# Feed-forward layers: one load of 512 moving columns for the high and low activations, in place of two of 256

## What is computed

```python
def _ffn(h, p):                                                # first stack
    return (jax.nn.silu(h @ p['w_ff_gate']) * (h @ p['w_ff_up'])) @ p['w_ff_down']

gate, up = jnp.split(h2 @ w_gate_up[l], 2, axis=-1)            # second stack
x = x + (jax.nn.silu(gate) * up) @ w_down[l]
```

## Time and profile before

| what | value |
|---|---|
| median of 3 runs | 2888.91 us (2883.22 to 2889.05) |
| the profiled execution's own time | 2887.15 us |
| its span, first to last instruction | 2885.4 us |
| TensorE matmul / weight load, busy share | 93% / 89% |
| VectorE / ScalarE, busy share | 71% / 53% |
| mean granted TensorE clock | 0.962 of full |

### The profile page before, as it was taken

The page is one execution under the profiler, slowest core; times in us unless marked ns, Lnnn a source line. Parts: engine busy times, 40 slices in busy tenths (PEclk is TensorE's granted clock), DMA queues, the critical chain, the costliest instruction groups (busy, mean ns, idle before and its releaser), DMA issues.

```text
span 2885.4 us, 66260 instructions
## 1 busy us (share of the span) xinstructions
PE 2691.2 (93%) x27300; PEld 2555.8 (89%) x27300; DVE 2037.8 (71%) x3675; ACT 1518.7 (53%) x3207; POOL 0.2 (0%) x4
## 2 busy tenths in 40 slices
PE   7989899999989899899989898999999899998998
PEld 5988889999988779799989887798998689996998
DVE  4987878688778887666658788877665665565655
ACT  4555355655655346454565453465445555455554
POOL 0000000000000000000000000000000000000000
PEclk9999999999999999999999899999999999999999
DMA  8453445455554334355434433344554145541554
GB/s 297 151 190 131 140 151 183 144 177 185 165 178 146 132 125 161 119 190 185 151 97 161 147 113 114 104 151 174 183 186 136 63 133 178 187 160 38 165 184 157
DMA packets 120500, 442.32 MB, mean 153 GB/s; under 512 B 13296, under 2 KB 15472, under 8 KB 118816
## 3 DMA queue, kind: packets, MB, share of 16 engines
q1 hardware_dynamic: 108416, 392.86, 40.7%
q10 hardware_dynamic: 11808, 45.42, 4.6%
HBM read 437.18 MB, written 1.05 MB: 152 GB/s over the span
## 4 chain that ended last, share of the span: by engine, by line
PE 67%; DVE 20%; ACT 6%; DMA 3%; issue 2%; SPq 0%; ACTq 0%; DVEq 0%
PE lin L462 17%; PE lin L463 17%; PE lin L464 17%; DVE arena L1869 5%; DVE w_lo L1709 5%; DMA w_raw<-in_stream 2%; ACT w_hi L1109 2%; PE lin L475 1%; PE lin L478 1%; PE lin L479 1%; DMA a_raw<-in_ada 1%; PE aux L580 1%; PE aux L663 1%; PE lin L513 1%; PE aux L642 1%
## 5 line engine op out<-in xcount | busy, mean ns | idle before, releaser
L1709 DVE TENSOR_TENSOR w_lo<-w_raw,w_hi 128x1024 fp32r<-128x1024 f32 x722 | 876.3, 1221 | 332.3 <-ACT w_hi L1109 326.7
L462 PE MATMUL lin<-h_hi,w_hi 128*128 128x256 f32 x3456 | 1001.3, 290 | 5.3 <-DVE h_lo L1805 2.9
L463 PE MATMUL lin<-h_lo,w_hi 128*128 128x256 f32 x3456 | 988.6, 286 | 0.0
L464 PE MATMUL lin<-h_hi,w_lo 128*128 128x256 f32 x3456 | 988.0, 286 | 0.0
L1109 ACT ACTIVATE w_hi<-w_raw 128x512 fp32r<-128x512 f32 x1446 | 828.8, 623 | 261.1 <-DMA w_raw<-in_stream 164.5
L462 PEld LDWEIGHTS lin<-h_hi,w_hi 128*128 128x128 f32 x3456 | 673.7, 195 | 15.8 <-issue 5.3
L463 PEld LDWEIGHTS lin<-h_lo,w_hi 128*128 128x128 f32 x3456 | 673.6, 195 | 0.2
L464 PEld LDWEIGHTS lin<-h_hi,w_lo 128*128 128x128 f32 x3456 | 672.9, 195 | 0.0
L462 PE MATMUL lin<-s_hi,w_hi 128*128 128x256 f32 x1520 | 441.0, 290 | 11.1 <-DVE s_lo L1805 4.5
L464 PE MATMUL lin<-s_hi,w_lo 128*128 128x256 f32 x1520 | 432.6, 285 | 0.5 <-issue 0.5
L463 PE MATMUL lin<-s_lo,w_hi 128*128 128x256 f32 x1520 | 433.1, 285 | 0.0
(11 more groups left out here) (279 smaller groups left out, 3495.5 us busy)
## 6 DMA issues: line engine op xcount, KB each, us to landing
w_raw<-in_stream SPq DMA_DIRECT2D x723, 512.0 KB, 3.6
a_raw<-in_ada ACTq DMA_DIRECT2D x80, 512.0 KB, 3.6
arena<-in_first SPq DMA_DIRECT2D x6, 1024.0 KB, 14.0
X<-in_tokens SPq DMA_DIRECT2D x2, 1024.0 KB, 13.5
s_f<-in_first SPq DMA_DIRECT2D x2, 1024.0 KB, 18.3
arena<-in_const ACTq DMA_DIRECT2D x1, 1856.0 KB, 10.2
arena<-in_small ACTq DMA_DIRECT2D x1, 1536.0 KB, 13.3
out<-arena SPq DMA_DIRECT2D x1, 1024.0 KB, 3.9
```

The lines of the kernel that those rows point to most:

```text
L462: used(pe.matmul(o, whi, hi[:, k, :], start=k == 0, stop=False), first)
L463: pe.matmul(o, whi, lo[:, k, :], start=False, stop=False)
L464: mm = pe.matmul(o, wlo, hi[:, k, :], start=False, stop=k == kcs - 1)
L1709: dve.tensor_tensor(w_lo[:, m % SLOTS, :], w_raw[:, m % RAW, :], w_hi[:, m % SLOTS, :].bitcast(F32), ALU.subtract).then_inc(sems["lo_ready ...
```

## The change

In four of the five feed-forward parts (passes two and four and both layers of the second stack) high and low activations lie in one tensor (`h_both`, `s_both`), and for each weight tile TensorE makes two matmuls: the high weights by both parts at once (512 columns, a whole bank), and the low weights by the high part (256 columns, into the bank's first half). What was one sum in a bank is now two halves, MAIN and CROSS, that have to be added. For a pair of chunks ScalarE copies both CROSS halves (512 elements), VectorE adds both MAIN halves to them and frees the two banks, and only then ScalarE applies SiLU, in place in SBUF. VectorE splits the product of a pair one pair later. For a down chunk VectorE does one more operation (CROSS out by ScalarE, MAIN added by VectorE, then the residual). The first pass keeps three products. Pairs need an even bank, so in pass four two dummy matmuls that keep the clock are now a chunk of the ring (`keep_clock_in_ring`), and ScalarE's `post` waits for it before its first operation. In every feed-forward part the running sum is now made in the second half alone.

```diff
...
+            def two_halves(o, both, k, last):
+
+                whi, wlo, first = weight()
+                mm = pe.matmul(o.rearrange("p (a t) -> p a t", a=2), whi, both[:, :, k, :], start=k == 0, stop=False)
+                return mm, first, pe.matmul(o[:, MAIN], wlo, both[:, 0, k, :], start=False, stop=last)
+
+            def dense_halves(both, ready=None, kcs=KC):
+
+                o = bank()
+                for k in range(kcs):
+                    if ready:
+                        pe.wait_ge(sems[ready[0]], ready[1] + k + 1)
+                    mm, first, end = two_halves(o, both, k, k == kcs - 1)
+                    used(mm, first)
+                done(end)
...
-            def post(l, x, b, squared=False):
-
-                warm()
+            def post(l, x, b, squared=False, ring=False):
+
+                if ring:
+
+                    arrived(0)
+                    moved(act.activation(small[:, 1, 14:15], c1("alpha")[:, 1:2], ACT.Sqrt))
+                else:
+                    warm()
...
+            def feed_forward_halves(gate, squared=None):
+                for i in range(2):
...
+                    for c in range(HALF):
+                        cross = arrived_pair()
+                        if c >= 2:
+
+                            act.wait_ge(sems["s_ready"], s0 + c - 1)
+                        act.activation(two_bufs[:, :, c % 2, :], cross, ACT.Copy).then_inc(sems["cross_moved"], 1)
+
+                        act.wait_ge(sems["lin_evac"], n.at("lin_evac"))
+                        act.activation(gate_buf[:, c % 2, :], gate_buf[:, c % 2, :], ACT.Silu).then_inc(sems["pair_silu"], 1)
+                        split_to(at.tile // TILES + SLOTS)
...
+            def residual_halves(x, alpha, gate, means, early):
+
+                for c in range(KC):
+                    lows_for(1)
+                    o, buf = at.next_bank(), gate_buf[:, c % 2, :]
+                    dve.wait_ge(sems["cross_moved"], at.up("cross_moved"))
+                    if gate is None:
+                        ins = dve.tensor_tensor(buf, o[:, MAIN], buf, ALU.add)
+                    else:
+                        ins = dve.scalar_tensor_tensor(buf, o[:, MAIN], gate(c), buf, ALU.mult, ALU.add)
+                    ins.then_inc(sems["lin_evac"], 1)
+                    dve.wait_ge(sems["lin_evac"], at.up("lin_evac"))
+                    dve.scalar_tensor_tensor(x[:, c, :], x[:, c, :], alpha, buf, ALU.mult, ALU.add).then_inc(sems["r_ready"], 1)
...
+            def feed_forward_halves(x, gate):
...
+                    for c in range(HALF):
+                        lows_for(2)
+                        main, pair, y = at.next_pair(MAIN), two_bufs[:, :, c % 2, :], y_buf[:, c % 2, :]
+                        dve.wait_ge(sems["cross_moved"], at.up("cross_moved"))
+                        dve.tensor_tensor(pair, main, pair, ALU.add).then_inc(sems["lin_evac"], 2)
+                        dve.wait_ge(sems["lin_evac"], at.up("lin_evac", 2))
+                        if c:
+                            split_product(c - 1)
+                        dve.wait_ge(sems["pair_silu"], at.up("pair_silu"))
+                        step(dve.tensor_tensor(y, gate_buf[:, c % 2, :], y, ALU.mult))
+                    split_product(HALF - 1)
...
```

More of the change, by code:

```diff
@@ L339, in v2, with bank_pair @@
             return vec2[:, at:at + 1]
-        lin = [ctx.enter_context(nc.psum_tensor(f"lin{i}", [P, 512], F32)) for i in range(4)]
+        lin_banks = ctx.enter_context(nc.psum_tensor("lin", [P, 4, 512], F32))
+        lin = [lin_banks[:, i, :] for i in range(4)]
+        def bank_pair(b, cols):
+            assert b % 2 == 0
+            return lin_banks[:, b:b + 2, cols]
+        MAIN, CROSS = slice(0, S), slice(S, 2 * S)
         aux = [ctx.enter_context(nc.psum_tensor(f"aux{i}", [P, 512], F32)) for i in range(4)]
@@ L465, in dense, with dense_halves_together @@
                 done(mm)
+            def two_halves(o, both, k, last):
[10 more added lines that the diff above has]
+                done(end)
+            def dense_halves_together(chunks, ready):
+                banks, start = [bank() for _ in range(chunks)], at.tile
+                for k in range(KC):
+                    pe.wait_ge(sems[ready[0]], ready[1] + k + 1)
+                    for c, o in enumerate(banks):
+                        at.tile = start + c * KC + k
+                        mm, first, end = two_halves(o, h_both, k, k == KC - 1)
+                        used(mm, first if c == 0 else k == KC - 1)
+                        if k == KC - 1:
+                            done(end)
             def dense_together(chunks, ready):
@@ L606, in keep_clock, with keep_clock_in_ring @@
                     pe.matmul(aux[3][:, 0:S], c1("mean1024"), const1[:, 0:S], start=True, stop=True)
+            def keep_clock_in_ring(k):
+                o = bank()
+                for _ in range(k):
+                    mm = pe.matmul(o[:, 0:S], c1("mean1024"), const1[:, 0:S], start=True, stop=True)
+                done(mm)
             def head_columns(name, heads, chunks):
@@ L693, in feed_forward @@
                     for c in range(KC):
-                        dense(s_hi, s_lo, ("s_ready", s0) if c == 0 else None, kcs=HALF)
+                        ready = ("s_ready", s0) if c == 0 else None
+                        if halves:
+                            dense_halves(s_both, ready, kcs=HALF)
+                        else:
+                            dense(s_hi, s_lo, ready, kcs=HALF)
                     n.up("r_ready", KC)
-                    n.up("sum_ready")
+                n.up("sum_ready")
             def gates(l):
@@ L962, in _ @@
                     else:
-                        keep_clock(2)
+                        if turn == 3:
+                            keep_clock_in_ring(2)
+                        else:
+                            keep_clock(2)
                         variance_columns(M)
@@ L976, in _ @@
                     n.up("h_ready", KC)
-                    feed_forward()
+                    feed_forward(turn > 0)
                     if turn == 3:
@@ L1117, in arrived, with arrived_pair @@
                 at.tile_done = at.tile
+                if at.freed_elsewhere:
+                    act.wait_ge(sems["lin_evac"], n.at("lin_evac"))
+                    at.freed_elsewhere = False
                 n.up("lin_evac")
                 return at.next_bank()
+            def arrived_pair():
+                for _ in range(2):
+                    at.tile += KC
+                    split_to((at.tile - 1) // TILES + SLOTS)
+                    act.wait_ge(sems["lin_done"], at.up("lin_done"))
+                    at.tile_done = at.tile
+                n.up("lin_evac", 2)
+                return at.next_pair(CROSS)
             def moved(ins):
@@ L1834, in residual @@
                         early(c)
+            def residual_halves(x, alpha, gate, means, early):
+                for c in range(KC):
+                    lows_for(1)
[3 more added lines that the diff above has]
+                        ins = dve.tensor_tensor(buf, o[:, MAIN], buf, ALU.add)
+                    else:
+                        ins = dve.scalar_tensor_tensor(buf, o[:, MAIN], gate(c), buf, ALU.mult, ALU.add)
+                    ins.then_inc(sems["lin_evac"], 1)
+                    dve.wait_ge(sems["lin_evac"], at.up("lin_evac"))
+                    dve.scalar_tensor_tensor(x[:, c, :], x[:, c, :], alpha, buf, ALU.mult, ALU.add).then_inc(sems["r_ready"], 1)
+                    n.up("r_ready")
+                    if means and c >= 1:
+                        dve.wait_ge(sems["r_ready"], at.now("r_ready"))
+                        ins = dve.tensor_tensor(std[:, 1, :], std[:, 1, :] if c > 1 else x[:, 0, :], x[:, c, :], ALU.add)
+                        if c < KC - 1:
+                            step(ins)
+                        else:
+                            ins.then_inc(sems["sum_ready"], 1)
+                            n.up("sum_ready")
+                    early(c)
@@ new lines, in feed_forward_halves, with split_product @@
+            def feed_forward_halves(x, gate):
+                scaled = gate is not None
+                def split_product(c):
+                    both_parts(s_hi[:, c, :], s_lo[:, c, :], y_buf[:, c % 2, :], "s_ready")
+                dve.wait_ge(sems["lin_evac"], n.at("lin_evac"))
+                at.bank = n.at("lin_evac") % 4
+                for i in range(2):
+                    for c in range(HALF):
[9 more added lines that the diff above has]
+                    split_product(HALF - 1)
+                    dve.wait_ge(sems["r_ready"], at.now("r_ready"))
+                    residual_halves(x, ALPHA if scaled and i == 0 else 1.0, gate, scaled and i == 1, lambda c: None)
+                dve.wait_ge(sems["r_ready"], at.now("r_ready"))
@@ L1849, in feed_forward @@
                     dve.wait_ge(sems["r_ready"], at.now("r_ready"))
```

(2 more changed lines are left out.)

60 lines of the change are left out of this document (45 added, 15 removed).

## The result

The changed kernel takes 2868.41 us in the median of 4 runs (2863.09 to 2870.81), beside 2888.98 (2883.22 to 2890.86) for the kernel before on the same chip: a ratio of 0.9934, with a 95% interval of 0.9919 to 0.9948. That is 20.6 us less. The forecast was 2849, 40 us less: the sign was right and the size twice too large. 2868 is what the first rival gave. The profiled execution took 2863.09 us, with a span of 2861.3.

The account below looks back on a forecast made before the run. TensorE's matmul distances were taken to bound the kernel. -47.1 + 3.8 + 2.0 + 1.2 = -40.1 us from the profiled 2887.15 gave 2847.0; with the median 1.8 above that execution, 2849 us, range 2824 to 2872.

Parts of the forecast that it names:

- the first rival: Feed-forward tiles: each weight load adds its own 13.3 ns, wide matmul 0.227 us; 21.1 us less, 2868; chance 0.20.
- What bounds the kernel: Four feed-forward parts: TensorE is busy for all of 190 us at full clock; nobody else sets the pace.
- Two matmuls for three: Feed-forward tiles: wide 0.217, narrow 0.120, so 0.337 instead of 0.360 us; 2048 tiles, 47.1 us less.
- the four rows it stood on: Trace evidence on matmul distances: half clock, full clock at 0.120 us, 48 weight columns, and plain float32 dummies.
- From gate and up to down: First down chunk: TensorE waits at the eleventh tile for VectorE, 0.48 us eight times; 3.8 us more.
- Leaving a part: Last down chunk: one more VectorE operation before the residual, 0.51 us four times; 2.0 us more at most.
- Pass four's norm: Pass four: ScalarE's table load waits for the dummies, now a chunk of the ring; 1.2 us more.
- Costs beside TensorE and the handover: Chunk pairs: VectorE 4.27, ScalarE 3.55, loop 5.0 us fit within 5.39; rival of a longer loop: 2921, chance 0.10.
- The sum: Whole kernel: -47.1 + 3.8 + 2.0 + 1.2 = -40.1 us.

Follow-up runs that it names:

- three loads again: The changed kernel with the wide matmul cut back into two of 256 columns, three loads a tile, all else kept: 2888.10 us, ratio 0.9999 to the kernel before.
- TensorE alone: Runs without the reference's computation, in blocks of 64 matmuls of one kind at full clock: fp32r distances 0.1199, 0.1733 and 0.2267 us for 256, 384 and 512 columns.

## Why the prediction was wrong, by its own steps

**What bounds the kernel** was right: TensorE's distances, and nothing else. The saved matmul with its load moved the parts; everything else of the change together moved nothing that shows (three loads again: 0.9999).

**Two matmuls for three: the term that failed.** It took 0.217 for the wide matmul and 2048 x 0.023 = 47.1 us. Measured are 0.233 and 0.117, a saving of 13.3 or 6.7 ns a tile by its pace: 758 x 0.0133 + 1285 x 0.0067 = 18.7 us. The step that failed is the sentence that a load "fits nearly free into 213 ns, and does not quite fit into 107". TensorE alone shows the same 13.3 ns with 256, 384 and 512 columns, so nothing of it is hidden by a longer stream, and in the kernel the wide one stands at 0.230 to 0.241. Three of the four rows it stood on were of another kind. The dummies in plain float32 have another type, whose surplus is 2.7 ns. The half clock has no surplus for either form, as the first tiles of the last part show now, where the granted clock is 0.50:

```profile
2662.25 0.63 PE L487 MATMUL lin<-h_both,w_hi 128*128 128x512 f32 x1
2662.67 0.41 PE L488 MATMUL lin<-h_both,w_lo 128*128 128x256 f32 x1
2662.89 0.47 PE L487 MATMUL lin<-h_both,w_hi 128*128 128x512 f32 x1
```

Wide 0.42, narrow 0.22, together 768 columns at 1.2 GHz: at half clock the change gains nothing. And the 48 weight columns tell nothing of 128, since the surplus does not go with the columns loaded. The row that did count, 0.120 at full clock with the right type and load, gave the first rival: 13.3 ns for each load, 2868. Its mean is close; its constancy is not, since a tile of wide and narrow has two paces. That its 2868 was met so closely is in part luck: it had 27.3 us saved in the tiles and 6.2 given back, where 18.7 and 1.7 were measured.

**From gate and up to down: oversized.** Forecast 0.48 us eight times, 3.8. The chain, second stack, VectorE, ScalarE and TensorE:

```profile
2394.88 0.40 PE L487 MATMUL lin<-s_both,w_hi 128*128 128x512 f32 x1
...
2395.08 0.60 ACT L1320 ACTIVATE two_bufs<-lin 128x512 f32<-128x512 f32 x1 [1.68 <-PE lin L488]
2395.78 0.69 DVE L1990 TENSOR_TENSOR two_bufs<-lin,two_bufs 128x512 f32<-128x512 f32 x1 [1.00 <-ACT two_bufs L1320]
...
2397.17 0.42 DVE L1995 TENSOR_TENSOR two_bufs<-two_bufs 128x256 f32<-128x256 f32 x1
2397.62 0.29 DVE L1921 CAST s_both<-two_bufs 128x256 fp32r<-128x256 f32 x1
2397.95 0.42 DVE L1922 TENSOR_TENSOR s_both<-two_bufs,s_both 128x256 fp32r<-128x256 f32 x1
...
2398.43 0.50 PE L487 MATMUL lin<-s_both,w_hi 128*128 128x512 f32 x1
2398.77 0.28 PE L488 MATMUL lin<-s_both,w_lo 128*128 128x256 f32 x1
```

The last part is ready at 2398.37, 3.49 after the first down tile's start; the forecast had 3.59. But the eleventh tile comes later than forecast, at 10 x 0.353 = 3.53, and TensorE, which has just worked, starts 0.06 behind VectorE and not 0.26. Its next start is 0.34 later instead of 0.23. The eleventh tile's distance from the tenth and the twelfth's from it are together 0.12 to 0.19 us longer than two at 0.353; over all eight stalls that is 1.2 us.

**Leaving a part: 2.0 forecast at most, 0.5 measured.** It shows in pass four alone, where the mean's first matmul starts 2176.52 - 2174.56 = 1.96 us after ScalarE takes out the last chunk, beside 1.45 before. In the second stack ScalarE's squares wait behind a weight split in either kernel; in pass two the next low part is waited for either way (3.08 and 3.10 us from last start to next).

```profile
2174.56 0.47 ACT L1331 ACTIVATE two_bufs<-lin,mod 128x256 f32<-128x256 f32 x1 [1.38 <-PE lin L488]
...
2175.07 0.48 DVE L1962 SCALAR_TENSOR_TENSOR two_bufs<-lin,mod,two_bufs 128x256 f32<-128x256 f32 x1
2175.59 0.42 DVE L1965 SCALAR_TENSOR_TENSOR X<-X,two_bufs 128x256 f32<-128x256 f32 x1
...
2176.52 0.70 PE L737 MATMUL aux<-std,const 128*128 128x256 f32 x2 [2.00 <-DVE std L1969]
```

**Pass four's norm: 1.2 forecast, nothing measured.** The table load does not wait for the ring's dummies, the last of which ends at 1969.73; the wait stands at the operation behind it, in answer to the earlier trace rows:

```profile
1968.53 1.28 ACT L1260 ACT_TABLE_LOAD   x1 [0.30 <-issue]
1969.83 0.20 ACT L1260 ACTIVATE small<-const 128x1 f32<-128x1 f32 x1
1969.94 0.61 ACT L1227 ACTIVATE M<-arena 128x512 f32<-128x512 f32 x1
```

From table load to squares it is 1.41 us, and 1.40 before.

**Costs beside TensorE and the handover: right.** The groups, answering to the earlier trace rows:

```profile
L1990 DVE TENSOR_TENSOR two_bufs<-lin,two_bufs 128x512 f32<-128x512 f32 x88 | 60.7, 690 | 64.7 <-ACT two_bufs L1320 64.7
...
L1320 ACT ACTIVATE two_bufs<-lin 128x512 f32<-128x512 f32 x88 | 52.5, 596 | 115.0 <-PE lin L488 115.0
...
L1323 ACT ACTIVATE two_bufs<-two_bufs 128x256 f32<-128x256 f32 x88 | 36.7, 418 | 75.0 <-DVE two_bufs L1990 74.6
```

690, 596 and 418 ns, where 690, 600 and at most 460 were taken. ScalarE's exits wait for TensorE, never TensorE for a bank.

**The sum.** -18.7 + 1.2 is -17.5, and the tiles behind the first 16 of each part did become faster by that, from 735.8 us in all four to 718.4. The other 1.5 us of the -19.0 lie at the starts of the parts: the first 16 tiles took 25.6 us in all four before and 24.1 after. In the kernel before, the clock granted over the first three us was 0.63 in pass four and 0.80 in layer one of the second stack; after, it was 1.00 in both. The saved load has no part in that: with the columns laid out side by side pass four began at 0.66 again. With the 0.5 for leaving a part it is -18.5. The medians' 20.6 lies 2 us off, within the runs' scatter. The profiled execution is 24.1 less. The other 5.6 us lie outside the four parts: 2.5 less ahead of the first, 6.2 less between passes two and four, and 3.1 more behind pass four, where the granted clock was 0.92 before and 0.89 after. How much of these the change brought about is not shown.

## What to carry to other kernels

When a row is used as evidence for what another instruction costs, it must agree with it in type, load and clock; a block of 64 of the very instruction costs one short run and settles it. Making one fp32r matmul out of two, with one full weight load less and the same columns, was worth 7 to 13 ns here at the full clock and nothing at half clock. Mixing types within a stream undid the gain; a cheaper type for whole stretches was not tried in the kernel.

## What the runs showed of the hardware that was not expected

- A stream of wide and narrow fp32r matmuls in turn has two stable paces, 0.3467 and 0.3533 us a tile, and keeps the one it starts with: in one stretch for 260 tiles, with VectorE, ScalarE and DMA at work beside it. An extra matmul can change it. One of 384 columns left the faster pace in 12 of 12 trials alone and for 2011 of 2025 tiles in the kernel. Why that length does it stays open.
- The surplus of an fp32r matmul at full clock goes in steps and not with the weight columns: 6.7 ns with 112, 80, 64 and 32, 9.3 with 96, 10.5 with 48 and 13.3 with 128, all with 256 columns moved.
- Between fp32r and bf16 matmuls in turn the bf16 weights were loaded 0.32 us behind the start of the wide matmul, and not with it: a pair of 512 and 256 columns takes 0.364 us and not 0.347.
